# Depthwise convolution of 31 taps: one of eight tiles moves to GpSimd, and the shared tile is divided anew between VectorE and TensorE

## The reference, cut to what matters

```python
def conv_module(h, w_pw1, w_dw, b_dw, ln_g, ln_b, w_pw2):
    u = h @ w_pw1
    a, gate = jnp.split(u, 2, axis=-1)
    u = a * jax.nn.sigmoid(gate)
    u = lax.conv_general_dilated(          # depthwise, 31 taps, 15 of padding
        u, w_dw[:, None, :].astype(u.dtype), window_strides=(1,),
        padding=[(CONV_PAD, CONV_PAD)], dimension_numbers=('NWC', 'WIO', 'NWC'),
        feature_group_count=D_MODEL) + b_dw
    u = jax.nn.silu(layer_norm(u, ln_g, ln_b))
    return u @ w_pw2
```

## Time and profile before

| what | value |
|---|---|
| median of three runs | 2249.67 us |
| the profiled execution's own time | 2251.57 us |
| its span on the core | 2249.5 us |
| PE busy, share of the span | 2159.5 us, 96% |
| DVE busy | 1498.7 us, 67% |
| ACT busy | 930.5 us, 41% |
| POOL busy | 43.6 us, 2% |
| stretch of the taps, from the first gating to the end of the sums | about 62 to 238 us |

### The profile page before, as it was taken

The page is one execution under the profiler, slowest core; times in us unless marked ns, Lnnn a source line. Parts: engine busy times, 40 slices in busy tenths (PEclk is TensorE's granted clock), DMA queues, the critical chain, the costliest instruction groups (busy, mean ns, idle before and its releaser), DMA issues.

```text
span 2249.5 us, 39556 instructions
## 1 busy us (share of the span) xinstructions
PE 2159.5 (96%) x15976; PEld 1888.0 (84%) x15976; DVE 1498.7 (67%) x2399; ACT 930.5 (41%) x1448; POOL 43.6 (2%) x37
## 2 busy tenths in 40 slices
PE   6999999999999999999999989999999999899997
PEld 3655678888888589999998987789989999688997
DVE  4779674444455866676667785586686677656666
ACT  3225532222233744454444453344454453344444
POOL 0000000000003000000001100000000000000000
PEclk9999999999999999999999999999999999999999
DMA  7768323223223045556554311355546554143663
GB/s 289 272 247 304 106 82 103 95 94 103 94 85 103 1 161 194 192 166 203 194 190 152 129 58 50 103 177 191 193 158 195 190 177 141 57 141 122 196 195 122
DMA packets 93556, 338.89 MB, mean 151 GB/s; under 512 B 10224, under 2 KB 12400, under 8 KB 93168
## 3 DMA queue, kind: packets, MB, share of 16 engines
q1 hardware_dynamic: 92096, 331.84, 44.3%
q10 hardware_dynamic: 1328, 5.21, 0.6%
HBM read 335.96 MB, written 1.05 MB: 150 GB/s over the span
## 4 chain that ended last, share of the span: by engine, by line
PE 84%; DVE 8%; ACT 4%; DMA 2%; issue 1%; SPq 0%; DVEq 0%; ACTq 0%
PE ps L556 21%; PE ps L558 21%; PE ps L557 21%; PE ps L964 2%; PE ps L663 2%; DMA ring<-weights 2%; PE ps L1235 1%; DVE WS L2062 1%; PE ps L579 1%; ACT HS L1831 1%; PE ps L911 1%; ACT WS L1518 1%; PE ps L1046 1%; PE ps L1069 1%; PE ps L921 1%
## 5 line engine op out<-in xcount | busy, mean ns | idle before, releaser
L2062 DVE TENSOR_TENSOR WS<-ring,WS 128x1024 fp32r<-128x1024 f32 x484 | 593.3, 1229 | 339.1 <-ACT WS L1518 338.3
L556 PE MATMUL ps<-HS,WS 128*128 128x256 f32 x2928 | 809.9, 277 | 7.3 <-DVE WS L2062 4.5
L558 PE MATMUL ps<-HS,WS 128*128 128x256 f32 x2928 | 806.0, 275 | 0.0
L557 PE MATMUL ps<-HS,WS 128*128 128x256 f32 x2888 | 794.7, 275 | 0.0
L1518 ACT CAST WS<-ring 128x1024 fp32r<-128x1024 f32 x484 | 506.6, 1049 | 545.8 <-PE ps L558 454.2
L556 PEld LDWEIGHTS ps<-HS,WS 128*128 128x128 f32 x2928 | 549.7, 188 | 11.2 <-DVE WS L2062 4.6
L558 PEld LDWEIGHTS ps<-HS,WS 128*128 128x128 f32 x2928 | 549.7, 188 | 0.0
L557 PEld LDWEIGHTS ps<-HS,WS 128*128 128x128 f32 x2888 | 542.2, 188 | 1.0 <-issue 1.0
L556 PE MATMUL ps<-CH,WS 128*128 128x512 f32 (+1 forms) x464 | 176.5, 380 | 0.3 <-DVE WS L2062 0.3
L557 PE MATMUL ps<-CH,WS 128*128 128x512 f32 (+1 forms) x464 | 173.9, 375 | 0.0
L558 PE MATMUL ps<-CH,WS 128*128 128x512 f32 (+1 forms) x464 | 173.8, 375 | 0.0
(11 more groups left out here) (422 smaller groups left out, 2674.6 us busy)
## 6 DMA issues: line engine op xcount, KB each, us to landing
ring<-weights SPq DMA_DIRECT2D x630, 512.0 KB, 3.5
X<-xs ACTq DMA_DIRECT2D x1, 2048.0 KB, 8.9
con<-const ACTq DMA_DIRECT2D x1, 2016.0 KB, 9.4
X<-mem ACTq DMA_DIRECT2D x1, 1024.0 KB, 5.6
y<-X SPq DMA_DIRECT2D x4, 256.0 KB, 2.2
vecs<-vec SPq DMA_DIRECT2D x1, 311.5 KB, 7.6
con<-const SPq DMA_DIRECT2D x1, 130.0 KB, 8.7
```

What stands on the lines that cost most here:

```text
L556: pe.matmul(dst, w[0][:, cut], upper, start=first, stop=False, skip_group_check=True)
L557: pe.matmul(dst, w[0][:, cut], lower, start=False, stop=False, skip_group_check=True)
L558: return pe.matmul(dst, w[1][:, cut], upper, start=False, stop=last, skip_group_check=True)
L2062: dve.tensor_tensor(WS[:, split % HALVES, 1, :], ring[:, panel % RING, :], WS[:, split % HALVES, 0, :].bitcast(F32), ALU.subtract).then_in ...
```

## The change

One of VectorE's tiles, tile 3 (`POOL_TILE`), goes to GpSimd in full. GpSimd does a tap in two instructions: a multiply of the shifted window by the tap's weight into one of two buffers (`SCALED`), and an addition of that buffer to `CV[:, 3]`; the first tap is one multiply with the bias added. That makes 31 multiplies and 30 additions of 128x512, begun when `glu3` is done, and each instruction waits on GpSimd's own counter for the ones that it depends on. VectorE's part of the shared tile rises from 12 taps to 25, TensorE's falls from 19 to 6, so that TensorE has 37 taps in all. VectorE's order of tiles becomes (0, 1), (2, 4), (5, 6), where the last pair has 31 taps of tile 5 and 25 of tile 6, so 180 taps in all. The order of the sums over the tiles changes with it: tile 3's sum stands after pair 19.

```diff
 GATE_TAPS, LOWER_TAPS = 10, 5
-SHARED_TAPS = 12
+SHARED_TAPS = 25
+POOL_TILE = 3
 CONV_TILES = 6
...
+        SCALED = area(20480, 2, CHUNK)
...
-            order = [*range(CONV_TILES - 2), CONV_TILES + 1, CONV_TILES - 2, CONV_TILES - 1, CONV_TILES]
-            sums_at = {6: order[0:2], 16: order[2:4], MOD_PAIRS: order[4:]}
+            order = [0, 1, 2, 4, POOL_TILE, CONV_TILES + 1, CONV_TILES - 1, CONV_TILES]
+            sums_at = {6: order[0:2], 16: order[2:4], 19: order[4:5], MOD_PAIRS: order[5:]}
+            conv_by = lambda k: "pool" if k == POOL_TILE else "dve" if k <= CONV_TILES else "act"
...
-            taps = [(tap, j) for j0 in range(0, CONV_TILES, 2) for tap in range(TAPS) for j in (j0, j0 + 1)]
-            taps[-2 * SHARED_TAPS:] = [(tap, j) for tap in range(SHARED_TAPS) for j in (CONV_TILES - 2, CONV_TILES - 1, CONV_TILES)]
-            shift = TAPS - SHARED_TAPS
-            taps[-3 * SHARED_TAPS:] = [(tap + shift * (j < CONV_TILES), j) for tap, j in taps[-3 * SHARED_TAPS:]]
+            taps = [(tap, j) for pair in ((0, 1), (2, 4), (5, CONV_TILES)) for tap in range(TAPS) for j in pair
+                    if j < CONV_TILES or tap < SHARED_TAPS]
...
+            own = CV[:, POOL_TILE, :].rearrange("p (g t) -> p g t", g=2)
+            scaled = lambda tap: SCALED[:, tap % 2, :].rearrange("p (g t) -> p g t", g=2)
+
+            def scale(tap):
+
+                if tap >= 3:
+                    pool.wait_ge(pool_done, at("pool", f"tap{tap - 2}"))
+                s.step(pool.tensor_scalar(scaled(tap), U[:, POOL_TILE, :, tap:tap + T], v("dw", tap * KT + POOL_TILE), None,
+                                          ALU.mult).then_inc(pool_done, 1), f"scaled{tap}")
+
+            pool.wait_ge(inputs_in[1], 16)
+            pool.wait_ge(dve_done, at("dve", f"glu{POOL_TILE}"))
+            s.step(pool.tensor_scalar(own, U[:, POOL_TILE, :, 0:T], v("dw", POOL_TILE), v("dw_b", POOL_TILE), ALU.mult,
+                                      ALU.add).then_inc(pool_done, 1), "tap0")
+            scale(1)
+            for tap in range(1, TAPS):
+                if tap + 1 < TAPS:
+                    scale(tap + 1)
+                pool.wait_ge(pool_done, at("pool", f"scaled{tap}"))
+                pool.wait_ge(pool_done, at("pool", f"tap{tap - 1}"))
+                s.step(pool.tensor_tensor(own, own, scaled(tap), ALU.add).then_inc(pool_done, 1), f"tap{tap}")
+            plan["pool", f"conv{POOL_TILE}"] = s.n
```

More of the change, by code:

```diff
@@ L737, in diagonal_tap @@
                 s.step(ins.then_inc(pe_done, 1), f"tap{n}")
-            order = [*range(CONV_TILES - 2), CONV_TILES + 1, CONV_TILES - 2, CONV_TILES - 1, CONV_TILES]
-            sums_at = {6: order[0:2], 16: order[2:4], MOD_PAIRS: order[4:]}
+            order = [0, 1, 2, 4, POOL_TILE, CONV_TILES + 1, CONV_TILES - 1, CONV_TILES]
+            sums_at = {6: order[0:2], 16: order[2:4], 19: order[4:5], MOD_PAIRS: order[5:]}
+            conv_by = lambda k: "pool" if k == POOL_TILE else "dve" if k <= CONV_TILES else "act"
             def mean_sums(n):
                 for k in sums_at.get(n, ()):
-                    pe.wait_ge(*after("dve" if k <= CONV_TILES else "act", f"conv{k}"))
+                    pe.wait_ge(*after(conv_by(k), f"conv{k}"))
                     ins = pe.matmul(ps[:, 3, :], ones, CV[:, k, :], start=(k == order[0]), stop=(k == order[-1]), skip_group_check=True)
```

## The result

The changed kernel takes 2268.47 us in the median (2268.02 to 2270.17) against 2249.32 for the kernel before: **19 us slower**, a ratio of 1.0089 (95% interval 1.0076 to 1.0101). The profiled execution has 2270.17 us, 18.6 above that of before. The forecast was 2279, slower by 29, from 2262 to 2296.

A forecast was written before the change was run, and what follows sets the result against it. VectorE and TensorE end together, the DMA close behind. VectorE's 110.0 us plus 53.9 of GpSimd's 55.9 from 102.1 put `conv6` at 266.0 and the sum at 267.1 against 238.2, 28.9 us later: 2279 us, range 2262 to 2296.

The forecast's parts named there:

- What bounds the stage: From 157.3 to 234.75 us: VectorE and TensorE end together, the DMA close behind; after the change VectorE ends last.
- Reads shut each other out, turn by turn: Beside the taps: VectorE and GpSimd, reading SBUF, alternate and stop each other for whole instructions; 61 instructions cost 55.9 us.
- The price of an addition: GpSimd's 30 additions on tile 3: each costs VectorE 1.14 us, together 34.2 us.
- The price of a multiply: GpSimd's 31 multiplies on tile 3: each costs VectorE 0.70 us, between 0.40 and 1.14, together 21.7 us.
- A multiply at line rate: GpSimd's multiplies: by the skill they would be near the lower end, 0.40 us, and the sum some 8 us smaller.
- VectorE's other terms: From `glu3` to `conv6`: 110.0 us besides GpSimd's; fewer taps save 11.7, unpartnered tile 5 taps add 0.7, idle 3.8 + 7.6 goes.
- The last sums: Behind `conv6`: one sum instead of up to four, 0.93 us; a granted-clock dip costs nothing while VectorE ends last.
- `glu7` and TensorE: `glu7` near 199 us in place of 157, then 19.4 MB of panels in 55 us; TensorE through at some 256 us.
- the rival without exclusion: GpSimd and VectorE don't shut each other out on taps; sums end near 229.5 us, total 2241 us; chance 0.08.
- VectorE kept no port: Rival at the taps: GpSimd gets in only where VectorE pauses, so TensorE waits at pair 19; 2296 us; chance 0.07.
- The half-way rival: Beside the taps only GpSimd's additions shut VectorE out, its multiplies cost nothing; 2262 us; chance 0.06.
- the two slower rivals: At the taps: VectorE keeps the port, 2296 us, chance 0.07; only additions shut it out, 2262 us, chance 0.06.

The follow-up runs named there:

- half panels: Only the left half of the last 43 w_mod panels loaded: on the kernel before, 2248.58 us; on the changed kernel with only GpSimd's first tap, 2236.25 us.
- the writing kernel: Changed kernel with GpSimd's 60 further instructions on tile 3 replaced by 60 clearings of 128x2048, which read nothing: 2249.85 us, ratio 0.9997.
- the half-panels kernel: Changed kernel with only GpSimd's first tap, and only the left half of the last 43 w_mod panels loaded: 2236.25 us, ratio 0.9938.
- the kernel without GpSimd's work: Changed kernel with 60 of GpSimd's 61 instructions on tile 3 left out, only its first tap computed: 2248.04 us, ratio 0.9994.

## Why the prediction was right, and where it was off

- **What bounds the stage.** Right that VectorE, TensorE and the stream end together, and that VectorE would be last after the change. The half panels show the stream and VectorE as the two that count; TensorE's own work would have been through 4 us sooner (72.0 us after `glu7` in place of 76.4).
- **Reads shut each other out, turn by turn.** Right, on the grounds of rows of other instructions; the taps do the same, and by the writing kernel it hangs on reading SBUF. The rule of the Trainium skill ("SBUF — State Buffer", "Who interferes with whom") agrees in this too: it excepts a GpSimd instruction that only writes, and beside 60 of those the taps took 0.743 us. That the two shut each other out for the whole instruction is not what the multiplies show: the tap lost 0.44 us to an instruction of 1.56 to 1.89. The measurement decides.
- **The price of an addition.** 1.14 us taken, 1.04 measured. To the delay of a stopped split (0.91 and 1.01 us) the prediction had added what GpSimd's row had already run (0.23 and 0.13); in the train the delay alone is what a tap costs, 1.04 by starts and 1.03 by lengths (1.77 less 0.74).
- **The price of a multiply.** The term of VectorE's sum that was most off: 0.70 taken, 0.44 measured, near the lower end of 0.40. I had taken its length for the time in which it holds VectorE; it lasts 1.56 us or more and holds VectorE for 0.44. The two prices together make 44.8 us instead of 55.9, which is the 11 us by which VectorE came earlier than forecast (254.5, not 266.0).
- **A multiply at line rate.** The Trainium skill, "GPSIMD Engine Reference", "Engine selection", calls one-input instructions there roughly line-rate, which would have put the multiply near the lower end. The hold agrees with that (0.44 us); the duration of 1.56 us for 512 elements does not.
- **VectorE's other terms.** Right: 42.3 - 11.7 (18 taps less) - 11.4 (idle time) + 0.7 (lone taps) = 19.9 us; measured from `glu3` to `conv6`, 152.4 against 132.65, 19.8.
- **The last sums.** 2.4 us less were expected. Two sums took 3.78 us, as long as four before, so only 0.4 us were won. TensorE had waited 7.2 us for VectorE, and the granted clock in the window from 250 to 260 us was 0.66 of 2.4 GHz on average, so 1.2 GHz for part of it: the two sums lost about 1.9 us to it (3.78 less half of 3.70), just where I had said that it costs nothing. In the half-panels kernel, where TensorE had waited 0.45 us, two sums took 1.98.
- **`glu7` and TensorE.** Forecast near 199, measured 171.5. With the multiplies letting VectorE through, three taps and not two fall on one of GpSimd's, and GpSimd ends at 210.5 and not at 200. TensorE needed 73.2 us from `glu7` to its last tap and not 57; it was through at 244.7, where I had 256, and two errors hid each other. The same mistake made the rival without exclusion too fast: it had 2241, and the kernel without GpSimd's work has 2248. The term was the stream. The forecast had 19.4 MB left behind `glu7`, the rival 23.6 MB, both at a full 350 GB/s; after the change 317 GB/s over 73.2 us are 23.2 MB, so there was more to load and the rate was lower. In the nine kernels with whole panels in which TensorE doesn't wait for GpSimd's tile, it ran at 298 to 317 GB/s from `glu7` to the last tap. TensorE's own work, put at about the same 55 us, was too low as well: with half panels it took 63.2 us from `glu7` to the last tap.
- **The other rivals.** VectorE kept no port: GpSimd got in after each tap that it met. The half-way rival, with multiplies that cost nothing, had 2262 and was nearer to the 2268 than the likeliest case, since a multiply costs so little. The chances of the forecast and of the two slower rivals add up to 0.92 (0.79, 0.07 and 0.06), where 0.90 was written.

## What to carry to other kernels

Before giving elementwise work to GpSimd, look at what VectorE does at that time. If VectorE's instructions read two operands from SBUF and GpSimd's read SBUF too, price GpSimd's instruction by what it adds to VectorE's starts, and compare that with VectorE doing the work itself: here 1.48 against 0.66 us a tap, so that a tap moved was a loss wherever VectorE had no idle time to hide it. And where an engine is relieved, ask first what else ends at the same time: 13 taps less on TensorE and some 11 us less on VectorE gave nothing, because the stream of panels ended there too.

## What the runs showed of the hardware beyond that

A GpSimd instruction's length is not the time for which it stops VectorE: a multiply of 128x512 by a scalar lasts 1.56 us beside a gating and 1.78 to 1.89 beside taps, and stops a tap for 0.44; an addition lasts 1.27 and, beside taps, 1.50, and stops a tap for 1.04. Where both engines have work waiting they alternate: three taps in 3.46 us to one multiply and one addition.

Clearings by GpSimd left the taps alone but not VectorE's first taps (L2226, one SBUF operand and scalars). In the writing kernel, two ahead of the clearings and two beside them:

```profile
73.22 0.99 DVE L2226 TENSOR_SCALAR arena<-arena,vecs 128x512 f32<-128x512 f32 x2
...
132.77 3.88 DVE L2226 TENSOR_SCALAR arena<-arena,vecs 128x512 f32<-128x512 f32 x2
```

One takes 0.54 us alone, 2.0 on average beside the clearings (four of the six in that kernel; 1.53 is the average of all six), and 1.2 beside the multiplies and additions. The Trainium skill names such an instruction in "SBUF — State Buffer", "Who interferes with whom", as one that can take both ports; the rows agree with it. With the change only two of them run beside GpSimd, which doesn't count here.
